# Turning the probabilities of the dilated attention on VectorE and GpSimd instead of TensorE

## The chip, the cores and the metric

One Trainium2 chip, one core. The metric is the device time of one execution in microseconds (us); lower is better. TensorE (PE in the profile), VectorE (DVE), ScalarE (ACT), GpSimd (POOL) and SyncE (SP, which issues the loads of weights) each run a program of their own and meet at semaphores.

## The reference, cut to what matters

Two layers over 256 tokens of width 2048, all in float32: one latent-attention layer (MLA), then one dilated sliding-window layer with three branches (dilation 1, 4, 16) and 16 heads of width 128. The change lies in the second. For each head:

```python
s = jnp.einsum('brnqhe,brnkhe->brnhqk', qs, kb)
s = jnp.where(valid, s * (E ** -0.5) + alibi, NEG_INF)
m = jnp.max(s, axis=-1, keepdims=True)
p = jnp.exp(s - m)
den = jnp.sum(p, axis=-1)
o = jnp.einsum('brnhqk,brnkhe->brnqhe', p, vb) / den
...
wts = jax.nn.softmax(jnp.stack(lses, axis=-1), axis=-1)      # over the three branches
o = jnp.einsum('bshge,bshg->bshe', jnp.stack(outs, axis=3), wts)
return h + (o * jax.nn.silu(gate)) @ w_o
```

The kernel merges the three branches into one softmax over 384 columns per query (256 of the dense branch, 64 of each dilated one), which is the same sum.

## The kernel before, in words

**The bulk.** Nearly all of the time is projections of the 256 tokens by float32 weights. Each weight step (128 x 1024 numbers, 512 KB) is loaded by SP into a ring of four slots, `raw`; ScalarE rounds it to a high part (`highs`, L486), VectorE subtracts to get the low part (`lows`, L837), and TensorE multiplies high and low parts in three matmuls for each product (L1327), 12 matmuls of 512 columns a step. `raw_full`, `hi_ready`, `lo_ready` and `slot_used` carry a slot from engine to engine. Step n + 4 is loaded when step n's low part is done, and rounded when TensorE has used step n.

**The dilated layer.** It runs over 8 pairs of heads, 40 steps (20 "quarters" of two steps) a pair. While pair i is projected, the attention of pair i - 1 runs between its quarters; the attention of the last pair runs between the steps of the output projection, at the steps in `B_LAST_SLOTS`. A pair has four units u (head by 128-query tile). `b_units(s)` says which stage of which unit belongs to quarter s: stage k of unit u in quarter 2 + u + k. So units follow each other one quarter apart, and each has four stages:

- stage 0: TensorE makes the scores (`b_score`, L1571 and L1576) into the bank `score`; VectorE adds the ALiBi table and takes the row maximum (`band_mask`, L929, two instructions of 64 rows, then L934); ScalarE takes the exponential in place in `prob` with the row sum (`unit_exp`, L540);
- stage 1: VectorE takes the reciprocal of the sum (`unit_den`, L965, called by `b_gates` ahead of the quarter's `lows`); ScalarE scales the probabilities (L738); TensorE turns them in three 128x128 blocks into the bank `turn` (`band_turn`, `turn_rows`, L1359); ScalarE copies the bank to `probT` (`unit_turned`, L524);
- stage 2: TensorE multiplies by the values (`band_pv`, L1591 and L1595) at the end of the quarter, ahead of that quarter's turn and score; VectorE multiplies with the gate (`band_out`, L954);
- stage 3: ScalarE and VectorE split the result into high and low part (`band_store` L814, `band_low` L961).

`prob` has two buffers, by u % 2; `probT`, `turn`, `score` and the bank of the product have one.

**The order on each engine** is written out by hand. In quarter s VectorE runs `b_gates`, `lows` of step 4 + 2s, the attention of the quarter (stage 3, 2, 0), the sums and rows of the norms (`chain_sums` L888 and L893, `b_rows` L907), the block turns of queries and keys (L1238), `lows` of step 5 + 2s. ScalarE runs `highs` of step 4 + 2s, the attention, the squares (L517), `highs` of step 5 + 2s. GpSimd has next to nothing: one power for each norm (`chain`, L434; in quarters 3, 7, 11 and 19 of a pair) and once a pair the halving of the ALiBi table (`halve`, L464, quarter 13).

**In the MLA layer** ScalarE carries 16 turned blocks of the keys of each pair to their partitions (L674), in batches that `KEY_MOVES` fixes: so many at MLA step 3, 4, 7 and 8 (step 8 is step 0 of the next pair), the last of which raises `key_turned`. TensorE waits for that in step 3 of the next pair.

Of the kernel before, what the change touches and what calls it, by code (L numbers as in the profile page):

```python
# [76 lines left out]
UNITS = 4  # L77
B_UNIT_0 = UNITS * PAIRS

B_ROUND_0 = 4 + 6 * PAIRS  # L80


def mla_round(i, k):

    return i * 6 - 1 + k
# [20 lines left out]
            for stage in (3, 2, 1, 0) if 0 <= s + 8 * (back - 1) - 3 - stage < UNITS]  # L106


def b_round(i, k):

    return i * UNITS + (B_ROUND_0 - UNITS) + k


QUAD = P // 4


KEY_MOVES = {3: range(0, 3), 4: range(3, 6), 7: range(6, 9), 8: range(9, 16)}


def b_units(s):  # L120
# [40 lines left out]
def build_program(nc, xT, x_later, x_tok, identity, consts, alibis, gains, w_in, w_pe, w_kv, w_gate_first, w_gate, w_q, w_out_a, w_b, w_out_b, out_tok):  # L161
    ctx = ExitStack()
    with ctx:
        def sb(name, shape, dt=F32):
            return ctx.enter_context(nc.sbuf_tensor(name, shape, dt))
# [24 lines left out]
        gate = sb("gate", [P, 2, TILES, 2 * P])  # L190
        rows = sb("rows", [P, 2, TILES, 512])
        prob = sb("prob", [P, 2, 512])
        probT = sb("probT", [P, 512])
        q_ropes = (qT[:, 2 * 512:3 * 512], v[:, 2 * 512:3 * 512])
        og = sb("og", [P, 2, P])
        out = sb("out", [P, 2, P])
# [141 lines left out]
        pv_ready = sem("pv_ready")  # L338
        og_ready = sem("og_ready")
        prob_scaled = sem("prob_scaled")  # L340
        gate_turned = sem("gate_turned")
        og_turned = sem("og_turned")
        o_ready = sem("o_ready")
# [75 lines left out]
        @block.gpsimd  # L419
        def _(pool):  # L420
            nc.gpsimd.memset(mhalf[:], -0.5).then_inc(set_up, 1)
            nc.gpsimd.memset(half[:], 0.5).then_inc(set_up, 1)
            for q_rope in q_ropes:
                nc.gpsimd.memset(q_rope, 0.0).then_inc(set_up, 1)
            pool.wait_ge(set_up, SET_UPS)

            def stream_rms(g):
                pool.wait_ge(x_mean, g + 1)
                nc.gpsimd.tensor_tensor(r[:], x_ms[:], mhalf[:, 0:TILES], ALU.pow).then_inc(r_ready, 1)

            def chain(c, width):

                pool.wait_ge(means, c + 1)
                nc.gpsimd.tensor_tensor(rms[:, 0:width], ms[:, 0:width], mhalf[:, 0:width], ALU.pow)\  # L434
                    .then_inc(rms_ready, 1)


            stream_rms(0)
            chain(0, TILES)
            chain(1, TILES)  # L440

            for i in range(0, PAIRS):
                for s in range(MLA_STEPS):
                    if s == 1:
                        chain(i * 2 + MLA_CHAIN_0, 2 * TILES)
                    if s == 7:
                        chain(i * 2 + (MLA_CHAIN_0 + 1), 2 * TILES)
            pool.wait_ge(loaded, 48)
            pool.sem_inc(alibi_ready, 1)

            def b_pair(i, attend):
                for s in range(B_QUARTERS):
                    if not attend and s == 2:
                        stream_rms(1)
                    for k, (_, at, units) in enumerate(B_CHAINS):
                        if s == at:
                            chain(i * 4 + (B_CHAIN_0 + k), units * TILES)
                    if attend and s == 13:
                        halve(i - 1)

            def halve(i):

                pool.wait_ge(mask_done, i * UNITS + (B_UNIT_0 + UNITS))
                nc.gpsimd.tensor_tensor(phase[:], phase[:], half[:].broadcast_to([P, N_PHASE]), ALU.mult)\  # L464
                    .then_inc(alibi_ready, 1)

            b_pair(0, False)
            for i in range(1, PAIRS):
                b_pair(i, True)


        @block.scalar
        def _(act):
# [252 lines left out]
            def b_attend(i, s):  # L726

                if s == 0:
                    act.wait_ge(blocked, (i - 1) * 4 + 3)
                    gain_of(kT, 2, gn("k_group"))  # L730
                for stage, u in b_units(s):
                    U = (i - 1) * UNITS + (B_UNIT_0 + u)
                    if stage == 3:
                        band_store((i - 1) * UNITS + u, i - 1, u)
                    if stage == 1:
                        act.wait_ge(den_ready, U + 1)
                        at = prob[:, u % 2, 0:BAND]
                        nc.scalar.activation(at, at, ACT.Copy, scale=den_inv[:, u:u + 1]).then_inc(prob_scaled, 1)  # L738
                        unit_turned(b_round(i, u), u, BAND)
                    if stage == 0:  # L740
                        unit_exp(U, u, BAND)

            def query_moves(i, part, parts):

# [87 lines left out]
        def _(dve):  # L832
# [89 lines left out]
            def band_mask(U, B, u, bias, iteration):  # L922

                dve.wait_ge(scored, U + 1)
                if u == 0:
                    dve.wait_ge(alibi_ready, iteration + 1)
                dve.sem_inc(mask_begun, 1)
                for rows_at, first in ((slice(0, HP), P), (slice(HP, P), 0)):
                    last = nc.vector.tensor_tensor_reduce(  # L929
                        out=prob[rows_at, u % 2, 0:BAND], in0=score[rows_at, first:first + BAND], in1=bias[rows_at],  # L930
                        scale=1.0, scalar=-3e38, op0=ALU.add, op1=ALU.max, accum_out=top[rows_at, u:u + 1])
                last.then_inc(mask_done, 1)
                dve.wait_ge(mask_done, U + 1)
                nc.vector.tensor_scalar(top_neg[:, u:u + 1], top[:, u:u + 1], -1.0, None, ALU.mult)\  # L934
                    .then_inc(top_ready, 1)
# [277 lines left out]
                    stream_lows(H_TURNED_AT.index(k - 1))  # L1213
                lows(OUT_A_0 + 4 + k, OUT_A_0 + 4 + k)

            def b_gates(i, s):

                for stage, u in b_units(s):
                    if stage == 1:
                        U = (i - 1) * UNITS + (B_UNIT_0 + u)  # L1220
                        unit_den(U, u)

            def b_blocks(f, k, n):

# [15 lines left out]
            def b_attend(i, s, par_before):  # L1240
                if s == 0:
                    b_rows(i - 1, par_before, 3)
                    dve.wait_ge(rows_ready, i * 4 + B_CHAIN_0)
                    queries = rows[:, 1, :, 0:2 * P]
                    nc.vector.transpose(queries, queries).then_inc(blocked, 1)
                if s in (0, 1):
                    gate_turn(i, s)
                for stage, u in b_units(s):
                    U = (i - 1) * UNITS + (B_UNIT_0 + u)
                    if stage == 3:  # L1250
                        band_low(U, i - 1, u)
                    if stage == 2:
                        band_out(U, i, u)
                    if stage == 0:
                        band_mask(U, (i - 1) * UNITS + u, u, alibi[:, u // 2, u % 2], i - 1)

            def b_rows(i, par, k):
                f, _, units = B_CHAINS[k]
# [7 lines left out]
            def b_pair(i, par, attend):  # L1266
                for s in range(B_QUARTERS):
                    if attend:
                        b_gates(i, s)
                    lows((i, B_STEPS), B_0 + 4 + 2 * s)  # L1270
                    if not attend and s == 1:
                        stream_lows(HALF_FILLS - 2)
# [32 lines left out]
                b_pair(t * 2 + 3, 1, True)  # L1305
            for k in range(OUT_STEPS):
                if k + 1 in B_LAST_SLOTS:
                    b_gates(PAIRS, B_LAST_SLOTS.index(k + 1))
                if k in B_LAST_SLOTS:
                    b_attend(PAIRS, B_LAST_SLOTS.index(k), 1)  # L1310
                if k in OUT_FILL_END:
                    add_stream(OUT_FILL_END.index(k), OUT_B_0, OUT_B_FILL_0, OUT_FILLS)
                if k < OUT_STEPS - 4:
                    lows(OUT_B_0 + 4 + k, OUT_B_0 + 4 + k)
# [3 lines left out]
        def _(pe):  # L1318
# [74 lines left out]

            pe.wait_ge(warm_set, 1)
            for _ in range(WARM):
                nc.tensor.matmul(score[:], probT[:, 0:P], probT[:], start=True, stop=True)
            for n in range(2):
                pe.wait_ge(first_x_hi, n + 1)
                pe.wait_ge(first_hi, n + 1)
# [176 lines left out]
                    last = nc.tensor.matmul(outer, qT[:, col:col + P], kT[:, col:col + P], start=True, stop=True)  # L1576
                last.then_inc(scored, 1)

            def band_turn(U, u, rnd):

                pe.wait_ge(prob_scaled, U - B_UNIT_0 + 1)
                turn_rows(rnd, [(prob[:, u % 2, k * P:(k + 1) * P], k * P) for k in range(BAND // P)])

            def band_pv(U, B, u, rnd):

                h, t = u // 2, u % 2
                pe.wait_ge(turn_read, rnd + 1)
                pe.wait_ge(out_made, B)
                both = probT[:, 0:BAND].rearrange("p (a k) -> p a k", a=2)
                for tile in range(TILES):  # L1590
                    nc.tensor.matmul(pv.rearrange("p (a k) -> p a k", a=2), v[:, tile * 768 + h * P:tile * 768 + (h + 1) * P],  # L1591
                                     both[:, :, tile * P:tile * P + HP], start=tile == 0, stop=False, skip_group_check=True)
                for half, first in ((0, SEQ), (1, HP)):
                    col = t * 768 + (1 + half) * 256 + h * P
                    last = nc.tensor.matmul(pv[:, half * HP:(half + 1) * HP], v[:, col:col + P],  # L1595
                                            probT[:, first:first + HP], start=False, stop=True, skip_group_check=True)
                last.then_inc(pv_ready, 1)

            def b_attend(i, s):
                for stage, u in b_units(s):  # L1600
                    U = (i - 1) * UNITS + (B_UNIT_0 + u)
                    if stage == 2:
                        band_pv(U, (i - 1) * UNITS + u, u, b_round(i, u))
                    if stage == 1:
                        band_turn(U, u, b_round(i, u))
                    if stage == 0:
                        if u == 0:
                            pe.wait_ge(gained, i * 4)
# [147 lines left out]
```

## Time and profile before

| | us |
|---|---|
| median of 3 runs | 1400.31 (1400.23 to 1400.31) |
| the profiled execution, its own time | 1400.47 |
| its span in the trace | 1398.7 |
| PE busy | 1390.0 (99%) |
| DVE busy | 1038.6 (74%) |
| ACT busy | 784.0 (56%) |
| POOL busy | 101.5 (7%) |

The granted clock of TensorE is 1.0, full speed, in all of the span. The profiled execution is 0.16 us above the median, and its span 1.77 us below its own time. In the profile, "L837" is line 837 of the kernel; `w_lo<-raw,w_hi` names output and inputs; "x4" after a row of a timeline counts instructions that are shown as one, and what stands in brackets is the idle time of the engine ahead of it with what ended it. A pair of the dilated layer takes 117.8 us; the rows further down are taken from the pair whose attention lies between 843 and 880 us.

### The profile page before, as it was taken

The numbers are of one execution on the slowest core, as the hardware profiler recorded it, in microseconds if no ns is written. First come the engines' busy times: TensorE is split into PE (matmuls) and PEld (weight loads), VectorE is DVE, ScalarE is ACT, GpSimd is POOL, SyncE is SP. The second block draws the span as 40 slices with busy tenths as digits, with TensorE's granted clock in tenths as the row PEclk, the third lists the DMA queues.
The fourth block names the chain that finished last, engine by engine and source line by source line (L and its number), as shares of the span: only waits on it lengthen the run. The fifth ranks groups of instructions, "written<-read, shape, count | busy, mean of one in ns | idle before, by whom it ended". The sixth has DMA issues, their size and how long they took to land.

```text
span 1398.7 us, 17859 instructions
## 1 busy us (share of the span) xinstructions
PE 1390.0 (99%) x6584; PEld 1162.5 (83%) x6584; DVE 1038.6 (74%) x1825; ACT 784.0 (56%) x1288; POOL 101.5 (7%) x67
## 2 busy tenths in 40 slices
PE   9999999999999999999999999999999999999999
PEld 7888888888888888888888888888888888888787
DVE  6777777757677868777877886887787788688653
ACT  6577777746544654564465465446446545644642
POOL 0101001000010001000101100101010110010000
PEclk9999999999999999999999999999999999999999
DMA  9653444455556545645554654565555465456454
GB/s 356 233 174 133 162 143 140 163 187 177 183 182 211 180 156 178 209 156 180 190 185 149 199 188 157 178 209 166 161 191 192 150 196 194 151 180 198 164 167 149
DMA packets 71223, 252.40 MB, mean 180 GB/s; under 512 B 7904, under 2 KB 8288, under 8 KB 71136
## 3 DMA queue, kind: packets, MB, share of 16 engines
q1 hardware_dynamic: 70704, 249.95, 54.2%
q10 hardware_dynamic: 432, 1.31, 0.3%
q8 instruction: 52, 0.85, 0.2%
q14 instruction: 35, 0.29, 0.1%
HBM read 249.14 MB, written 2.10 MB: 180 GB/s over the span
## 4 chain that ended last, share of the span: by engine, by line
PE 94%; DVE 3%; ACT 2%; issue 1%; DMA 1%; SPq 0%; POOL 0%; DVEq 0%; ACTq 0%
PE acc L1327 86%; PE turn L1359 1%; PE score L1576 1%; DVE w_lo L837 1%; PE score L1571 1%; PE pv_bank L1591 1%; PE pv_bank L1371 1%; DVE ss L888 1%; PE score L1467 1%; PE score L1469 1%; PE pv_bank L1595 1%; DVE prob L929 1%; ACT rows L517 1%; DMA raw<-in_w_in 1%; ACT prob L738 0%
## 5 line engine op out<-in xcount | busy, mean ns | idle before, releaser
L837 DVE TENSOR_TENSOR w_lo<-raw,w_hi 128x1024 fp32r<-128x1024 f32 x463 | 573.3, 1248 | 201.9 <-ACT w_hi L486 198.0
L486 ACT ACTIVATE w_hi<-raw 128x1024 fp32r<-128x1024 f32 x463 | 482.3, 1050 | 363.4 <-PE acc L1327 355.3
L1327 PE MATMUL acc<-w_hi,xa_hi 128*128 128x512 f32 x956 | 378.5, 396 | 0.4 <-DVE w_lo L837 0.3
L1327 PE MATMUL acc<-w_hi,xa_lo 128*128 128x512 f32 x956 | 373.0, 390 | 0.0
L1327 PE MATMUL acc<-w_lo,xa_hi 128*128 128x512 f32 x956 | 372.6, 390 | 0.0
L1327 PE MATMUL acc<-w_hi,xb_hi 128*128 128x512 f32 (+1 forms) x640 | 249.5, 390 | 0.0
L1327 PE MATMUL acc<-w_hi,xb_lo 128*128 128x512 f32 (+1 forms) x640 | 245.9, 384 | 0.0
L1327 PE MATMUL acc<-w_lo,xb_hi 128*128 128x512 f32 (+1 forms) x640 | 245.6, 384 | 0.0
L1327 PEld LDWEIGHTS acc<-w_hi,xa_lo 128*128 128x128 f32 x956 | 179.4, 188 | 37.7
L1327 PEld LDWEIGHTS acc<-w_hi,xa_hi 128*128 128x128 f32 x956 | 179.7, 188 | 37.3 <-issue 0.9
L1327 PEld LDWEIGHTS acc<-w_lo,xa_hi 128*128 128x128 f32 x956 | 179.7, 188 | 35.8
L434 POOL TENSOR_TENSOR rms<-ms,mhalf 128x4 f32<-128x4 f32 (+2 forms) x50 | 73.1, 1462 | 1048.6 <-DVE ms L893 854.7
L1327 PEld LDWEIGHTS acc<-w_hi,xb_lo 128*128 128x128 f32 x640 | 120.1, 188 | 22.7
L1327 PEld LDWEIGHTS acc<-w_lo,xb_hi 128*128 128x128 f32 x640 | 120.3, 188 | 22.1
L1327 PEld LDWEIGHTS acc<-w_hi,xb_hi 128*128 128x128 f32 x640 | 120.3, 188 | 21.9
L1327 PE MATMUL acc<-w_hi,oT_hi 128*128 128x512 f32 x256 | 102.3, 400 | 0.0
L1327 PE MATMUL acc<-w_hi,oT_lo 128*128 128x512 f32 x256 | 100.0, 391 | 0.0
L1327 PE MATMUL acc<-w_lo,oT_hi 128*128 128x512 f32 x256 | 99.8, 390 | 0.0
L1238 DVE STREAM_TRANSPOSE kT<-rows 32x256 f32<-32x256 f32 (+1 forms) x256 | 94.5, 369 | 4.5
L540 ACT ACTIVATE prob<-prob,top_neg 128x128 f32<-128x128 f32 (+1 forms) x64 | 34.3, 536 | 93.0 <-DVE top_neg L934 70.9
L517 ACT ACTIVATE rows<-acc 128x512 f32<-128x512 f32 (+2 forms) x50 | 39.2, 783 | 34.3 <-PE acc L1327 34.0
L929 DVE CUSTOM_DVE_ANT_0 prob<-score,phase 64x384 f32<-64x384 f32 x64 | 35.5, 555 | 29.8 <-PE score L1576 29.4
(179 smaller groups left out, 1163.6 us busy)
## 6 DMA issues: line engine op xcount, KB each, us to landing
raw<-in_w_b SPq DMA_DIRECT2D x320, 512.0 KB, 3.8
raw<-in_w_out_a SPq DMA_DIRECT2D x32, 512.0 KB, 3.3
raw<-in_w_out_b SPq DMA_DIRECT2D x32, 512.0 KB, 3.3
raw<-in_w_gate SPq DMA_DIRECT2D x30, 512.0 KB, 3.6
raw<-in_w_kv SPq DMA_DIRECT2D x16, 512.0 KB, 4.3
raw<-in_w_in SPq DMA_DIRECT2D x15, 512.0 KB, 6.2
raw<-in_w_q SPq DMA_DIRECT2D x16, 384.0 KB, 3.0
res<-in_x_tok SPq DMA_DIRECT2D x4, 512.0 KB, 7.9
```

What stands on the lines that cost most here:

```text
L434: nc.gpsimd.tensor_tensor(rms[:, 0:width], ms[:, 0:width], mhalf[:, 0:width], ALU.pow)\
L486: nc.scalar.activation(w[0][:, s, 0:width], raw[:, s, 0:width], ACT.Copy).then_inc(hi_ready, 1)
L517: nc.scalar.activation(rows[:, buf, :, 0:width], acc[:, pair, :, 0:width], ACT.Square)\
L540: nc.scalar.activation(prob[:, u % 2, 0:width], prob[:, u % 2, 0:width], ACT.Exp, bias=top_neg[:, u:u + 1], accum_out=den[:, u:u + 1])\
L837: nc.vector.tensor_tensor(w[1][:, s, 0:width], raw[:, s, 0:width], w[0][:, s, 0:width].bitcast(F32), ALU.subtract).then_inc(lo_ready, 1)
L888: nc.vector.tensor_reduce(ss[:, 0, 0:n].rearrange("p (t u) -> p t u", t=TILES), rows[:, buf, :, 0:units * span].rearrange("p t (u d) -> p ...
L929: last = nc.vector.tensor_tensor_reduce(out=prob[rows_at, u % 2, 0:BAND], in0=score[rows_at, first:first + BAND], in1=bias[rows_at], scale ...
L1238: return nc.vector.transpose(dst, src)
L1327: last = nc.tensor.matmul(out, x(a), y(b), start=start and k == 0, stop=stop and k == 2, **more)
L1359: last = nc.tensor.transpose(turn[:, col:col + P], src, ident[:])
L1371: last = nc.tensor.matmul(pv, probT[:, k * P:(k + 1) * P], val, start=k == 0, stop=k == len(values) - 1)
L1467: nc.tensor.matmul(score[:, 0:n], qT[:, par * 512 + at:par * 512 + at + P], kT[:, k_0 + h * SEQ:k_0 + h * SEQ + n], start=True, stop=False)
```

## The change

The three transposes on TensorE and ScalarE's copy of their bank go. The reciprocal (`unit_den`) and the scaling move from stage 1 to stage 0, right behind the exponential. At the start of quarter 3 + u VectorE turns the 32x32 blocks of the unit's 128x384 probabilities in place (`prob_turns`), and GpSimd carries the turned blocks from `prob` to `probT` in 16 copies of 32 partitions x 96 elements (`prob_moves`), each from one group of 32 partitions to another. `probT` gets two buffers. `band_pv` waits for the copies (`prob_moved`), and so does the mask of the unit after next, which writes the same buffer of `prob`. GpSimd's copies stand ahead of the power of quarter 3. Apart from that, the batches of key moves in the MLA layer are cut anew: 1, 3, 4 and 8 blocks instead of 3, 3, 3 and 7.

```diff
-KEY_MOVES = {3: range(0, 3), 4: range(3, 6), 7: range(6, 9), 8: range(9, 16)}
+KEY_MOVES = {3: range(0, 1), 4: range(1, 4), 7: range(4, 8), 8: range(8, 16)}
...
-        probT = sb("probT", [P, 512])
+        probT = sb("probT", [P, 2 * BAND])
...
             def b_pair(i, attend):                       # GpSimd
                 for s in range(B_QUARTERS):
+                    for stage, u in b_units(s) if attend else ():
+                        if stage == 1:
+                            prob_moves(i, u)
...
                         if s == at:
+                            if attend and k < 2:
+                                pool.wait_ge(prob_moved, (i - 1) * UNITS + (1, UNITS)[k])
                             chain(i * 4 + (B_CHAIN_0 + k), units * TILES)
...
+            def prob_moves(i, u):
+
+                B = (i - 1) * UNITS + u
+                pool.wait_ge(rms_ready, i * 4 + B_CHAIN_0 + (1 if u and i < PAIRS else 0))
+                pool.wait_ge(prob_blocks, B + 1)
+                pool.wait_ge(pv_ready, B_UNIT_0 + B - 1)
+                tiles = prob[:, u % 2, 0:BAND].rearrange("p (t k) -> p t k", k=P)
+                turned = probT[:, u % 2 * BAND:(u % 2 + 1) * BAND].rearrange("p (t k) -> p t k", k=P)
+                for n in range(16):
+                    a, b = n // 4, n % 4
+                    last = nc.gpsimd.tensor_copy(turned[b * QUAD:(b + 1) * QUAD, :, a * QUAD:(a + 1) * QUAD],
+                                                 tiles[a * QUAD:(a + 1) * QUAD, :, b * QUAD:(b + 1) * QUAD])
+                last.then_inc(prob_moved, 1)
...
-                    if stage == 1:                       # ScalarE
+                    if stage == 0:
+                        unit_exp(U, u, BAND)
                         act.wait_ge(den_ready, U + 1)
                         at = prob[:, u % 2, 0:BAND]
                         nc.scalar.activation(at, at, ACT.Copy, scale=den_inv[:, u:u + 1]).then_inc(prob_scaled, 1)
-                        unit_turned(b_round(i, u), u, BAND)
-                    if stage == 0:
-                        unit_exp(U, u, BAND)
...
                 dve.wait_ge(scored, U + 1)               # VectorE, band_mask
                 if u == 0:
                     dve.wait_ge(alibi_ready, iteration + 1)
+                if B >= 2:
+                    dve.wait_ge(prob_moved, B - 1)
...
-            def b_gates(i, s):
+            def prob_turns(i, s):
 
                 for stage, u in b_units(s):
                     if stage == 1:
-                        U = (i - 1) * UNITS + (B_UNIT_0 + u)
-                        unit_den(U, u)
+                        dve.wait_ge(prob_scaled, (i - 1) * UNITS + u + 1)
+                        nc.vector.transpose(prob[:, u % 2, 0:BAND], prob[:, u % 2, 0:BAND]).then_inc(prob_blocks, 1)
...
                         band_mask(U, (i - 1) * UNITS + u, u, alibi[:, u // 2, u % 2], i - 1)
+                        unit_den(U, u)
...
-            def band_turn(U, u, rnd):                    # TensorE
-
-                pe.wait_ge(prob_scaled, U - B_UNIT_0 + 1)
-                turn_rows(rnd, [(prob[:, u % 2, k * P:(k + 1) * P], k * P) for k in range(BAND // P)])
-
-            def band_pv(U, B, u, rnd):
+            def band_pv(U, B, u):
 
                 h, t = u // 2, u % 2
-                pe.wait_ge(turn_read, rnd + 1)
+                pe.wait_ge(prob_moved, B + 1)
                 pe.wait_ge(out_made, B)
```

## Rows read from the trace of the kernel before

**Rows 1.** The page, part 1: busy time, share of the span and instructions of each engine.
```profile
PE 1390.0 (99%) x6584; PEld 1162.5 (83%) x6584; DVE 1038.6 (74%) x1825; ACT 784.0 (56%) x1288; POOL 101.5 (7%) x67
```

**Rows 2.** Waits of PE: us in total, times, longest us.
```profile
PE turn L1359 <- ACT prob L738: 3.3, 8, 1.7
```

**Rows 3.** Timeline of PE, one pair's attention: start us, us, engine, line, operation, idle.
```profile
856.13 0.61 PE L1591 MATMUL pv_bank<-probT,v 128*128 128x128 f32 x4
...
857.35 0.55 PE L1359 MATMUL turn<-ident,prob 128*128 128x128 f32 x3 [0.22 <-ACT prob L738]
...
864.11 0.61 PE L1591 MATMUL pv_bank<-probT,v 128*128 128x128 f32 x4
...
864.95 0.50 PE L1359 MATMUL turn<-ident,prob 128*128 128x128 f32 x3
865.28 0.60 PE L1571 MATMUL score<-kT,qT 128*128 128x256 f32 x2
...
871.65 0.61 PE L1591 MATMUL pv_bank<-probT,v 128*128 128x128 f32 x4
...
878.32 0.61 PE L1591 MATMUL pv_bank<-probT,v 128*128 128x128 f32 x4
```

**Rows 4.** Timeline of DVE in the same pair.
```profile
844.33 0.55 DVE L929 CUSTOM_DVE_ANT_0 prob<-score,phase 64x384 f32<-64x384 f32 x1 [0.54 <-PE score L1576]
...
863.17 0.15 DVE L965 RECIPROCAL den_inv<-den 128x1 f32<-128x1 f32 x1
863.24 1.20 DVE L837 TENSOR_TENSOR w_lo<-raw,w_hi 128x1024 fp32r<-128x1024 f32 x1
864.37 0.28 DVE L961 TENSOR_TENSOR oT_lo<-out,oT_hi 128x128 fp32r<-128x128 f32 x1
...
866.51 0.55 DVE L929 CUSTOM_DVE_ANT_0 prob<-score,phase 64x384 f32<-64x384 f32 x1 [1.07 <-PE score L1576]
...
869.57 1.23 DVE L837 TENSOR_TENSOR w_lo<-raw,w_hi 128x1024 fp32r<-128x1024 f32 x1 [1.73 <-ACT w_hi L486]
```

**Rows 5.** Timeline of ACT in the same pair.
```profile
863.36 0.62 ACT L738 ACTIVATE prob<-prob,den_inv 128x384 f32<-128x384 f32 x1 [0.22 <-DVE den_inv L965]
...
867.88 0.62 ACT L540 ACTIVATE prob<-prob,top_neg 128x384 f32<-128x384 f32 x1 [1.90 <-DVE top_neg L934]
...
868.50 1.99 ACT L486 ACTIVATE w_hi<-raw 128x1024 fp32r<-128x1024 f32 x2
```

**Rows 6.** Timelines of POOL and DVE around the halving of the ALiBi table (L464).
```profile
903.69 1.23 DVE L837 TENSOR_TENSOR w_lo<-raw,w_hi 128x1024 fp32r<-128x1024 f32 x1
...
903.81 3.71 POOL L464 TENSOR_TENSOR phase<-phase,half 128x1536 f32<-128x1536 f32 x1
...
905.00 3.60 DVE L837 TENSOR_TENSOR w_lo<-raw,w_hi 128x1024 fp32r<-128x1024 f32 x1
```

**Rows 7.** Timeline of POOL: two memsets at the start, three powers in the same pair.
```profile
0.77 0.10 POOL L422 MEMSET half<- 128x1 f32 x1
0.81 0.53 POOL L424 MEMSET qT<- 128x512 f32 x1
...
855.52 2.55 POOL L434 TENSOR_TENSOR rms<-ms,mhalf 128x8 f32<-128x8 f32 x1 [25.92 <-DVE ms L893]
881.14 1.64 POOL L434 TENSOR_TENSOR rms<-ms,mhalf 128x8 f32<-128x8 f32 x1 [23.07 <-DVE ms L893]
902.84 1.01 POOL L434 TENSOR_TENSOR rms<-ms,mhalf 128x4 f32<-128x4 f32 x1 [20.06 <-DVE ms L893]
```

**Rows 8.** Groups of DVE, shapes apart: count | busy us, mean ns | idle before.
```profile
L1245 DVE STREAM_TRANSPOSE rows<-rows 128x512 f32<-128x512 f32 x8 | 5.7, 711 | 0.3
```

**Rows 9.** Timeline of PE in the last pair, beside the output projection.
```profile
1338.80 0.61 PE L1591 MATMUL pv_bank<-probT,v 128*128 128x128 f32 x4
...
1342.75 0.61 PE L1591 MATMUL pv_bank<-probT,v 128*128 128x128 f32 x4
```

**Rows 10.** Groups of ACT, shapes apart: count | busy us, mean ns | idle before.
```profile
L674 ACT ACTIVATE kT<-rows 32x128 f32<-32x128 f32 x128 | 39.3, 307 | 1.7
```

More of the change, by code:

```diff
@@ L78 @@
 B_UNIT_0 = UNITS * PAIRS
-B_ROUND_0 = 4 + 6 * PAIRS
 def mla_round(i, k):
@@ L106, in mla_units @@
             for stage in (3, 2, 1, 0) if 0 <= s + 8 * (back - 1) - 3 - stage < UNITS]
-def b_round(i, k):
-    return i * UNITS + (B_ROUND_0 - UNITS) + k
 QUAD = P // 4
-KEY_MOVES = {3: range(0, 3), 4: range(3, 6), 7: range(6, 9), 8: range(9, 16)}
+KEY_MOVES = {3: range(0, 1), 4: range(1, 4), 7: range(4, 8), 8: range(8, 16)}
 def b_units(s):
@@ L340, in build_program @@
         prob_scaled = sem("prob_scaled")
+        prob_blocks = sem("prob_blocks")
+        prob_moved = sem("prob_moved")
         gate_turned = sem("gate_turned")
@@ L469, in _ @@
                 b_pair(i, True)
+            for u in range(UNITS):
+                prob_moves(PAIRS, u)
         @block.scalar
@@ L1268, in b_pair @@
                     if attend:
-                        b_gates(i, s)
+                        prob_turns(i, s)
                     lows((i, B_STEPS), B_0 + 4 + 2 * s)
@@ L1307, in _ @@
                 if k + 1 in B_LAST_SLOTS:
-                    b_gates(PAIRS, B_LAST_SLOTS.index(k + 1))
+                    prob_turns(PAIRS, B_LAST_SLOTS.index(k + 1))
                 if k in B_LAST_SLOTS:
@@ L1395, in _ @@
             for _ in range(WARM):
-                nc.tensor.matmul(score[:], probT[:, 0:P], probT[:], start=True, stop=True)
+                nc.tensor.matmul(score[:], probT[:, 0:P], probT[:, 0:512], start=True, stop=True)
             for n in range(2):
@@ L1577, in b_score @@
                 last.then_inc(scored, 1)
-            def band_turn(U, u, rnd):
-                pe.wait_ge(prob_scaled, U - B_UNIT_0 + 1)
-                turn_rows(rnd, [(prob[:, u % 2, k * P:(k + 1) * P], k * P) for k in range(BAND // P)])
-            def band_pv(U, B, u, rnd):
+            def band_pv(U, B, u):
                 h, t = u // 2, u % 2
-                pe.wait_ge(turn_read, rnd + 1)
+                pe.wait_ge(prob_moved, B + 1)
                 pe.wait_ge(out_made, B)
-                both = probT[:, 0:BAND].rearrange("p (a k) -> p a k", a=2)
+                turned = probT[:, u % 2 * BAND:(u % 2 + 1) * BAND]
+                both = turned.rearrange("p (a k) -> p a k", a=2)
                 for tile in range(TILES):
@@ L1595, in band_pv @@
                     last = nc.tensor.matmul(pv[:, half * HP:(half + 1) * HP], v[:, col:col + P],
-                                            probT[:, first:first + HP], start=False, stop=True, skip_group_check=True)
+                                            turned[:, first:first + HP], start=False, stop=True, skip_group_check=True)
                 last.then_inc(pv_ready, 1)
@@ L1602, in b_attend @@
                     if stage == 2:
-                        band_pv(U, (i - 1) * UNITS + u, u, b_round(i, u))
-                    if stage == 1:
-                        band_turn(U, u, b_round(i, u))
+                        band_pv(U, (i - 1) * UNITS + u, u)
                     if stage == 0:
```

## The prediction, made before the changed kernel was run

> **What bounds the kernel now.** I began with the busy shares [rows 1]: PE is busy in 99% of the span, DVE in 74%, ACT in 56%, POOL in 7%. A busy PE is only a bound if it never waits, so the waits of PE came next [rows 2]: beside start-up, the one thing it waits for in 1398.7 us is the scaled probabilities ahead of a transpose, 8 times, 3.3 us in all, 1.7 of them once. The kernel is bound by TensorE's own work, and an instruction taken from PE shortens it, as long as nothing else becomes late. Then I read PE's, DVE's and ACT's timelines over one pair [rows 3 to 5], to price the transposes and to see when each step of a unit would be ready.
>
> **What goes.** On PE a unit's transposes take from 864.95 to the score at 865.28, 0.33 us, every other unit alike [rows 3]. There are 32 units: 28 in the seven pairs that run beside the next pair's projection give 28 x 0.33 = 9.2 us. In each of these pairs one transpose also waits 0.22 us (857.35) [rows 3], 7 x 0.22 = 1.5 us, which goes too. In the last pair the same removes 4 x 0.33 and the wait of 1.7 [rows 2], 3.0 us, but see the tail below. ScalarE's copy of the bank also goes, from an engine that has room.
>
> **What is late next.** PE's multiplication by the values, which now waits for GpSimd. One turn of a unit on PE is 864.11 to 871.65, 7.54 us; without the transposes 7.21 [rows 3].
>
> The ring on DVE and ACT, in starts. Mask to exponential 866.51 to 867.88, 1.37; exponential and read of its sum to reciprocal some 0.77 (0.62 and an estimate for the read); reciprocal to scaling 863.17 to 863.36, 0.19; scaling to ScalarE's next rounding 0.54 (its 0.62 less the usual overlap); a rounding to the low part it releases 868.50 to 869.57, 1.07; low part to DVE's next instruction 863.24 to 864.37, 1.13 [rows 4, 5]. Then comes the new block turn. The nearest row is the in-place turn of 128x512 in 711 ns [rows 8]; three quarters of it is 0.53, and I take 0.5 start to start; 0.71 is the upper end, which would shift the copies by 0.2. Then the low part of the next step, 1.13. So the copies can start 6.7 us after the unit's mask. With the 0.2 and 0.25 of `band_low` and `band_out` the ring closes in 7.2 us, which is just PE's 7.21: DVE doesn't fall behind, but it has nothing to spare in these quarters.
>
> Why the copies start only behind that low part: GpSimd and VectorE exclude each other here. One L837 takes 1.23 us; the next, issued at 905.00 while `halve` runs on POOL, takes 3.60, and `halve`, issued at 903.81 under the first, takes 3.71 [rows 6]. Ends fit one owner at a time: first L837 to 904.92, `halve` to 907.52, second L837 1.1 us on. The power of 855.52 takes 2.55 against 1.64 at 881.14 in the same way [rows 7]. After the block turn DVE goes straight into L837, so POOL waits.
> The Trainium skill ("SBUF — State Buffer", Who interferes with whom) says that a VectorE instruction with two SBUF inputs excludes a GpSimd one that reads SBUF, and one with a single such input does not. By that rule the copies would not slow masks, sums and block turns; if these were blocked too, each would wait one copy, 0.2 us, some 0.6 a unit in a ring without room, and three such units in each of 8 pairs would take back the whole gain. No row here tests this with a burst of copies.
>
> **The price of a copy.** No row shows one. Lower bound: the memsets start 0.04 apart and the 128x512 one takes 0.53, so 0.83 ns an element; 96 elements give 0.04 + 0.08 = 0.12 us [rows 7]. Upper: the powers of 4 and 8 columns take 1.01 and 1.64, 0.16 a column and 0.38 fixed [rows 7]; with `halve`'s 2.60 us for 1536 elements (1.7 ns each) [rows 6] a copy is 0.38 + 0.16 = 0.54. The nearest row is `halve`, plain arithmetic that reads SBUF: twice the memset's 0.83 x 1536 is 2.55 of its 2.60, so a reading instruction has a small fixed cost. I take 0.04 for dispatch, 0.08 for writing and as much for the read ahead of it, 0.20, and 16 x 0.20 = 3.2 us a unit; ends 1.9 and 8.6.
> The Trainium skill ("GPSIMD Engine Reference", Performance pitfalls) gives about 102 cycles for each read command that doesn't overlap the one before; an estimate by it is 0.21 us a copy, 3.3 a unit.
>
> **Does it fit?** Window from the earliest start of the copies to PE's need:
> - u0: mask 844.33, start 851.0; PE at 856.13 - 0.33 = 855.8: 4.8 us.
> - u1: mask 851.0; the squares, sums and means of the norm add 1.3, start 859.1. PE at 855.8 + 7.21 = 863.0: 3.9.
> - u2: mask 859.3, start 866.0; PE at 870.2: 4.2, less a collision with `band_low`.
> - u3: mask 866.5, start 873.2; PE at 870.2 + (878.32 - 871.65 - 0.33) = 876.5: 3.3 [rows 3, 4].
> 3.2 us fit everywhere, the last by a hair. No stall.
> Of the other waits: the power of quarter 3 now stands behind unit 0's copies (done 854.2; its means come at 856.3), hidden up to 5.3 us of copies; behind it wait DVE's L907 and all later `lows`. The mask's wait for the unit before last costs nothing at this size. The low part of 869.57 comes about 0.9 later, since scaling now precedes it; PE wants it at 871.65 + 1.17 + 2.7 = 875.5, so 4 us of cover remain; without it that 0.9 would be paid three times a pair. The halving is in quarter 13, clear of the copies. Key moves: as many as before, the last batch one longer, 0.31 us [rows 10], three steps ahead of PE's need: nothing; uncovered, 8 x 0.31 = 2.5. SP issues nothing new.
>
> **Tail.** In the last pair one step, not two, lies between the products of units 2 and 3: 1338.80 to 1342.75 [rows 9]. The window of 3.3 loses 2.7 and PE stalls 2.6 to 2.9, which eats that pair's 3.0. Net 0.1.
>
> **Sum:** 9.2 + 1.5 + 0.1 = 10.8 us off the profiled execution's 1400.47; the median is 0.16 lower, 1400.31, so 1389.5 to 1389.7: I say **1389.6**. With the lower bound of the copy the tail gives 1.2 more, 1388.4; with none of it in the way, 1387.
>
> **Rivals.**
> 1. *Copies somewhat dearer, 0.25 us (4.0 a unit).* u1 stalls 0.2, u3 0.6; 7 x 0.8 + 0.8 = 6.4; 1396. A reading instruction's fixed cost could be larger than `halve` lets through, since part of it may hide under the wait for the port.
> 2. *GpSimd becomes the bound: slower.* The place is PE's wait for `prob_moved` ahead of L1591. The point of decision is some 0.29 us a copy (4.6 a unit), where stalls eat the gain. At 0.30: 7 x 1.65 + 1.6 = 13.2, 1402.7. At 0.35 the copies of u1 run into the next L837 and lose 1.1 more: about 4 a pair, 31 in all, 1421. At the bound of 0.54 each unit takes 8.6 and two such collisions, some 18 a pair, 1530. For it: the powers' 0.38 fixed. Against: `halve`.
> 3. *The port is not handed over fairly.* If a burst of 16 keeps it, `band_low` and with it the mask wait up to 3.2 us and not 0.2. DVE's ring has no room, so the stall recurs at u2 and u3: 2 x 3 x 8 = 48, 1438. If instead each collision costs DVE 0.2 to 0.3, three times a pair, 7 us: 1397. Rows 6 show one owner after another, which speaks for turns.
> 4. *No effect:* the transposes' slots hid under weight loads. PE's starts are 0.33 later because of them [rows 3], so hardly.
>
> **How the numbers follow.** The forecast (copy up to 0.22) has 0.55; rival 1 and the mild form of 3 together 0.13; rival 2 0.24; rival 3's hard form 0.04; no effect 0.04. A measurement of this kernel can tell about 0.2% (2.8 us) from no change. Faster: 0.55 + 0.11 = 0.66; same: 0.02 of rivals 1 and 3, 0.01 of 2 at just 0.29, and 0.04, so 0.07; slower 0.27. The likeliest case's own range is 1387 to 1392. The range reaches from 1387 into rival 2 up to a copy of 0.35, 1421, leaving out about 0.17.
>
> **What would show it.** PE without L1359 in the dilated layer; L1591 with no wait but in the last pair; a pair of 116.3 instead of 117.8 us; POOL's group of 32x96 copies x512 at about 0.2 us start to start; L837 beside a copy longer by no more than one copy. Wrong if PE waits for POOL in every pair, or if DVE's masks start later each unit.

## The result and the profile after

The changed kernel takes 1431.67 us (median of 4 runs, 1430.06 to 1434.52) against 1400.28 before: ratio 1.0226, 95% interval 1.0212 to 1.024. It is 31 us slower; I had forecast 11 us faster and a range up to 1421. The profiled execution took 1430.06, its span is 1428.3.

First the shares of the engines and the page's costliest group on POOL, which was not there before [rows 1]:

```profile
PE 1396.4 (98%) x6488; PEld 1160.7 (81%) x6488; DVE 1056.9 (74%) x1857; ACT 768.0 (54%) x1256; POOL 277.2 (19%) x579
...
L470 POOL COPY probT<-prob 32x96 f32<-32x96 f32 x512 | 176.2, 344 | 206.4 <-issue 186.0
```

PE has 96 instructions fewer and is "busy" for longer; POOL is idle four fifths of the time. Neither share tells what happened. The waits of PE do (us in total, times, longest in us):

```profile
PE pv_bank L1603 <- POOL probT L470: 26.3, 16, 3.5
PE score L1412 <- POOL v L418: 1.8, 1, 1.8
PE acc L1343 <- DVE w_lo L850: 0.2, 1, 0.2
```

Where PE used to wait 3.3 us for the scaled probabilities [rows 2], it now waits 26.3 for the last copy of a unit. Next, PE's timeline over one pair, the first product by the values of each of the four units, as in [rows 3]:

```profile
865.31 0.71 PE L1603 MATMUL pv_bank<-probT,v 128*128 128x128 f32 x4
...
874.49 0.71 PE L1603 MATMUL pv_bank<-probT,v 128*128 128x128 f32 x4 [1.68 <-POOL probT L470]
...
883.48 0.61 PE L1603 MATMUL pv_bank<-probT,v 128*128 128x128 f32 x4
...
890.72 0.71 PE L1603 MATMUL pv_bank<-probT,v 128*128 128x128 f32 x4 [0.73 <-POOL probT L470]
```

The steps are 9.18, 8.99 and 7.24, where 7.97, 7.55 and 6.67 stood before and 7.21, 7.21 and 6.34 were forecast. The second step has no wait and is still 1.8 us too long; its cause is another one and comes below. POOL's timeline in the same pair shows why unit 1 and unit 3 are late (the rows with x16 are one unit's copies):

```profile
859.61 5.64 POOL L470 COPY probT<-prob 32x96 f32<-32x96 f32 x16 [20.47 <-issue]
866.06 2.49 POOL L428 TENSOR_TENSOR rms<-ms,mhalf 128x8 f32<-128x8 f32 x1 [0.81 <-DVE ms L906]
868.61 5.83 POOL L470 COPY probT<-prob 32x96 f32<-32x96 f32 x16
874.61 5.64 POOL L470 COPY probT<-prob 32x96 f32<-32x96 f32 x16 [0.17 <-issue]
883.11 7.55 POOL L470 COPY probT<-prob 32x96 f32<-32x96 f32 x16 [2.86 <-issue]
```

Unit 1's copies start at 868.61 behind the power and end at 874.44; PE goes on at 874.49. L850 is the subtraction for the low part, L837 before the change. Here are single copies of unit 1, and the L850 that one of them meets, in POOL's and DVE's timelines:

```profile
871.01 0.26 POOL L470 COPY probT<-prob 32x96 f32<-32x96 f32 x1
871.31 0.26 POOL L470 COPY probT<-prob 32x96 f32<-32x96 f32 x1
...
872.82 1.31 POOL L470 COPY probT<-prob 32x96 f32<-32x96 f32 x1
...
872.78 1.22 DVE L850 TENSOR_TENSOR w_lo<-raw,w_hi 128x1024 fp32r<-128x1024 f32 x1 [0.38 <-ACT w_hi L501]
```

A copy takes 0.26 us and the next starts 0.30 after its start. One that meets L850 takes 1.31, about 1.05 more, while L850 keeps its 1.22. So a unit takes 16 x 0.30 = 4.8 us and about 1 for each L850 it meets: one in unit 1, and three in unit 3, whose first copy is issued under an L850 (7.55 in all; the three copies concerned take 0.85, 0.92 and 0.98 more than 0.26).

The long second step is TensorE's clock. The rows are stretches of 1 us of this pair: their length, PE's busy time, the number of matmuls, the granted clock as a share of 2.4 GHz, and the DMA share with GB/s:

```profile
872.00:873.00 1.00, 0.81 (x4) 1.00 0.00 0
873.00:874.00 1.00, 0.00 (x0) 1.00 0.00 0
874.00:875.00 1.00, 0.51 (x4) 1.00 0.03 12
875.00:876.00 1.00, 1.00 (x8) 0.86 0.94 303
876.00:877.00 1.00, 1.00 (x6) 0.50 0.87 262
877.00:878.00 1.00, 1.00 (x4) 0.50 0.78 209
878.00:879.00 1.00, 1.00 (x4) 0.50 0.66 246
879.00:880.00 1.00, 1.00 (x5) 0.93 0.08 33
```

PE stood still for 1.68 us, up to 874.49; from 875.72 on the granted clock was 1.2 and not 2.4 GHz, for 3.4 us, which costs 1.7. Over the whole execution there are six such stretches of 3.4 us in the seven overlapped pairs and one of 6.8 around the last pair's first product, 27.3 us at half speed, some 13.5 us lost. The kernel before had none.

Put together, from the first product of the first pair to that of the last pair it is 844.2 us against 820.9 before, 23.3 more. With half the copies, the first experiment below, it is 806.8, so the transposes with the waits ahead of them were worth 14.0 there. The low clock adds 10.2. The remaining 27.1 are stalls of PE. Its waits for the copies hold 22.9 of them (without the last unit's), and a stall costs some 0.3 more than the idle time shown (the step of 9.18 is 1.94 over 7.24 with a wait of 1.68), which for 15 stalls fits the other 4.2. From the last pair's first product to the end it is 5.8 more than before, and 0.4 more up to the first product: 29.6 in all, the difference of the spans.

### The profile page after: what moved, and what is told of

It is laid out like the page before. It is cut to its first block, busy times and chain, and to the rows that moved or that the text cites. A ratio compares the mean times of both kernels' runs of the same rounds, so it can differ in the third digit from the quotient of the medians.

```text
span 1428.3 us, 18200 instructions
## 1 busy us (share of the span) xinstructions
PE 1396.4 (98%) x6488; PEld 1160.7 (81%) x6488; DVE 1056.9 (74%) x1857; ACT 768.0 (54%) x1256; POOL 277.2 (19%) x579
## 3 DMA queue, kind: packets, MB, share of 16 engines
q10 hardware_dynamic: 432, 1.31, 0.2%
## 4 chain that ended last, share of the span: by engine, by line
PE 79%; DVE 7%; POOL 6%; issue 4%; ACT 3%; DMA 1%; SPq 0%; DVEq 0%; ACTq 0%; POOLq 0%
PE acc L1343 73%; POOL probT L470 6%; DVE prob L944 2%; DVE w_lo L850 2%; ACT prob L555 1%; ACT w_hi L501 1%; PE pv_bank L1603 1%; PE pv_bank L1387 1%; DVE ss L901 1%; PE score L1483 1%; PE score L1485 1%; PE score L1592 1%; ACT rows L532 1%; PE score L1587 1%; DVE prob L1236 1%
## 5 line engine op out<-in xcount | busy, mean ns | idle before, releaser
L850 DVE TENSOR_TENSOR w_lo<-raw,w_hi 128x1024 fp32r<-128x1024 f32 x463 | 573.5, 1248 | 199.1 <-ACT w_hi L501 195.1
L1343 PE MATMUL acc<-w_hi,xa_hi 128*128 128x512 f32 x956 | 382.6, 400 | 0.4 <-DVE w_lo L850 0.2
L470 POOL COPY probT<-prob 32x96 f32<-32x96 f32 x512 | 176.2, 344 | 206.4 <-issue 186.0
```

Of the source, the lines that this page charges most:

```text
L470: last = nc.gpsimd.tensor_copy(turned[b * QUAD:(b + 1) * QUAD, :, a * QUAD:(a + 1) * QUAD], tiles[a * QUAD:(a + 1) * QUAD, :, b * QUAD:(b ...
L850: nc.vector.tensor_tensor(w[1][:, s, 0:width], raw[:, s, 0:width], w[0][:, s, 0:width].bitcast(F32), ALU.subtract).then_inc(lo_ready, 1)
L1343: last = nc.tensor.matmul(out, x(a), y(b), start=start and k == 0, stop=stop and k == 2, **more)
```

## The experiments

Before the runs I held **theory G** (G for GpSimd): only the copies' price was wrong, and everything follows from when their last one lands. **Rival R**: the ring of VectorE and ScalarE is the bound, since scaling and block turn now stand ahead of the low parts; then shorter copies help little.

### Half the copies

```diff
-                for n in range(16):
+                for n in range(0, 16, 2):
```

> The changed kernel with every second one of the 16 copies left out (half of the turned probabilities don't reach probT), all waits kept. Theory G (GpSimd's copies are the bound: 16 x 0.301 us start to start, 4.8 a unit, against windows of 3.9 and 3.3, each collision with L850 adding about 1 us): 8 x 0.30 = 2.4 us fit every window but the last pair's, PE doesn't wait for POOL in the first seven pairs, the granted clock stays 1.0 there, and the time is 1400.3 - 10.8 + 1.0 for the key moves - 0.8 for the shorter tail = about 1389.7 (1388 to 1391.5). Rival R (the ring of VectorE and ScalarE is the bound, since scaling and block turn now stand ahead of the low parts): half the copies change little of it, PE still waits in each pair, and the time stays above 1405.

Measured: **1390.98 us**, ratio 0.9933 (0.9919 to 0.9947). PE's timeline over the pair, then POOL's for units 1 and 3:

```profile
851.42 0.61 PE L1603 MATMUL pv_bank<-probT,v 128*128 128x128 f32 x4
...
858.66 0.61 PE L1603 MATMUL pv_bank<-probT,v 128*128 128x128 f32 x4
...
865.90 0.61 PE L1603 MATMUL pv_bank<-probT,v 128*128 128x128 f32 x4
...
872.25 0.61 PE L1603 MATMUL pv_bank<-probT,v 128*128 128x128 f32 x4
```

```profile
854.72 2.37 POOL L470 COPY probT<-prob 32x96 f32<-32x96 f32 x8
...
867.83 3.22 POOL L470 COPY probT<-prob 32x96 f32<-32x96 f32 x8 [3.88 <-issue]
```

The steps are 7.24, 7.24 and 6.35, within 0.03 of the forecast's 7.21, 7.21, 6.34. PE has no wait for the copies in seven pairs, and a pair takes 116.04 us against 117.77: the transposes and what hung on them are worth 1.73 a pair. The last pair stalls 3.1 us and then has 3.4 us at the low clock, some 1.6 us that this expectation had not counted and that account for the 1.3 above its 1389.7. Rival R falls: block turn, early scaling and all waits are as in the changed kernel, and PE never waits for them.

### Early scaling alone

The kernel before, with the reciprocal (VectorE) and the scaling (ScalarE) in stage 0; TensorE still turns.

```diff
-                    if stage == 1:
-                        act.wait_ge(den_ready, U + 1)
-                        ...scaling...
-                        unit_turned(b_round(i, u), u, BAND)
-                    if stage == 0:
-                        unit_exp(U, u, BAND)
+                    if stage == 1:
+                        unit_turned(b_round(i, u), u, BAND)
+                    if stage == 0:
+                        unit_exp(U, u, BAND)
+                        act.wait_ge(den_ready, U + 1)
+                        ...scaling...
...
                         band_mask(U, (i - 1) * UNITS + u, u, alibi[:, u // 2, u % 2], i - 1)
+                        unit_den(U, u)
```

> The kernel before with one part of the change alone: reciprocal and scaling in stage 0, right behind the exponential; TensorE still turns. Theory G: early scaling costs PE nothing and takes away the 8 waits of 3.3 us ahead of the transposes: about 1397.0 (1396 to 1398.5). Rival R: the later low parts make PE wait for L837, 1403 or more.

Measured: **1395.04 us**, ratio 0.9963 (0.9949 to 0.9976). It is faster by 5.3 and not by 3.3, below the range: a pair takes 117.31 instead of 117.77, so what shows as a wait of 0.22 us had cost 0.46, and in the same way the last pair's wait of 1.7 had cost 2.0 (from the seventh pair's first product to the last pair's it is 111.85 us instead of 114.27, and 0.46 of the difference is the seventh pair's own). This part of the change is a gain by itself, clear of the interval.

### The form of the copies, pair by pair

Pair 3 has four copies of 128x96, all partitions at once and each staying where it is; the other pairs change form or number:

```diff
+                if i == 3:
+                    for n in range(4):
+                        last = nc.gpsimd.tensor_copy(turned[:, :, n * QUAD:(n + 1) * QUAD], tiles[:, :, n * QUAD:(n + 1) * QUAD])
+                for n in {2: range(16), 3: (), 4: range(16), 5: range(1), 6: range(12), 7: range(8)}.get(i, range(16)):
...
+                    if i == 2:
+                        last = nc.gpsimd.tensor_copy(dst[:, 0], src[:, 0])
+                    elif i == 4:
+                        last = nc.gpsimd.memset(dst, 0.0)
```

> The changed kernel with another form of the copies in each pair (its output isn't the reference's from pair 2 on): pair 2 only a third of each copy (32x32), pair 3 four copies of 128x96 within the partitions, pair 4 memsets of 32x96 in their place, pair 5 one copy, pair 6 twelve, pair 7 eight, pairs 1 and 8 as they are. Prices, start to start: if the fixed part is what I mis-sized (0.04 assumed), 32x32 takes about 0.25 and 128x96 the same 0.30 as 32x96; if it is the rate, 32x32 takes 0.10 to 0.15. Memsets, which read nothing, take 0.12 each and don't wait for L850 if only the read port is shared; if they do wait, the first is about 1.1 us long. Pairs 5 and 7 run with no wait of PE for POOL and take 116.3 us between equal points; pair 6 (3.6 a unit) waits under 1 us in all; pairs 2 (4.0) and 6 thus lie between. Rival R: all pairs take about 120.5.

Measured: 1408.99 us (one run). POOL's timeline for unit 1, behind the power, of pairs 2, 3 and 4, then pair 5's one copy in unit 0 (issued under an L850) and in unit 1 (not), and pair 6's unit 3:

```profile
626.97 3.90 POOL L475 COPY probT<-prob 32x32 f32<-32x32 f32 x16
...
746.98 0.90 POOL L470 COPY probT<-prob 128x96 f32<-128x96 f32 x4
...
863.03 3.30 POOL L477 MEMSET probT<- 32x96 f32 x16
...
970.07 1.11 POOL L479 COPY probT<-prob 32x96 f32<-32x96 f32 x1 [20.46 <-issue]
...
979.07 0.26 POOL L479 COPY probT<-prob 32x96 f32<-32x96 f32 x1
...
1108.22 6.45 POOL L479 COPY probT<-prob 32x96 f32<-32x96 f32 x12 [2.66 <-issue]
```

32x32 costs 0.244 start to start and 32x96 0.301: 0.9 ns an element and 0.215 us besides, where I had assumed 1.7 ns and 0.04 us. That split holds for copies of 32 partitions. The copies of 128x96, which stay in their partitions and move four times as much each, start 0.21 apart, each before the one ahead has ended (0.27), and not the 0.30 that I expected: the same 128x384 numbers go in 0.90 us and not in 4.8. The change of partitions isn't what costs: of a unit's 16 copies four (those with a = b) stay in their group, and in the changed kernel these too start 0.30 apart from their neighbours. So the price hangs on the number of instructions, and on the 32 rows of each.

The memset of 32x96 takes 0.206, not the 0.12 that I had built from two memsets at the start [rows 7]; and its 16 take 3.30 us in every unit of pair 4, also where they begin under L850, while the one copy of pair 5 in that place takes 1.11. So what reads SBUF waits for L850, and what only writes does not. The Trainium skill ("SBUF — State Buffer", Who interferes with whom) says just this: a VectorE instruction with two SBUF inputs contends with a GpSimd one that reads SBUF, and not with one that only writes it. The trace agrees, with 1.11 us for the copy and 3.30 for the 16 memsets.

Pairs 3, 4 and 5 (and 7, with eight copies) have PE's steps of 7.24, 7.24, 6.35. Pair 6, with twelve, has 7.24, 7.24, 8.43: only unit 3 is late, by 2.1 us and not by the under 1 that I expected, since its copies meet three L850 (6.45 us for twelve). Pair 2 waits at unit 3 too (2.0 us).

### ScalarE carries a part

The whole computation again. GpSimd takes blocks 7 to 15, ScalarE 0 to 6 in its idle time ahead of the next exponential; key moves as before the change. The semaphore `prob_carried` is new; TensorE and the mask wait for it as well.

```diff
+                    if stage == 1:                       # ScalarE
+                        act.wait_ge(prob_blocks, B + 1)
+                        act.wait_ge(pv_ready, B_UNIT_0 + B - 1)
+                        for n in range(7):
+                            ... nc.scalar.activation(turned[...], tiles[...], ACT.Copy)
+                        last.then_inc(prob_carried, 1)
```

> The whole computation: ScalarE carries 7 of a unit's 16 blocks in its idle time ahead of the next exponential, GpSimd 9; key moves as before the change. Theory G: GpSimd 9 x 0.30 = 2.7 us, ScalarE 7 x 0.3 = 2.1 us beside it, both inside 3.3; PE waits in the last pair alone; 1400.3 - 10.8 - 0.5 = about 1389 (1387.5 to 1391), faster than the kernel before. Rival R: ScalarE is in the ring, so that its copies make it longer: slower than 1400. A middle case, ScalarE's copies delaying each exponential by some 0.2 us: 1391 to 1394.

Measured: **1393.20 us**, ratio 0.995 (0.9937 to 0.9962), faster than the kernel before but 2.2 us above its range. The steps are 7.24, 7.24 and 6.62, so ScalarE's copies make no step of units 0 to 2 longer. Unit 3 is late: it shows as a wait of 0.12 and costs 0.40 a pair (116.44 against 116.04 with half the copies), 7 x 0.40 = 2.8. The last pair stalls 3.4 us and has 3.4 us at the low clock. POOL's row for unit 3:

```profile
868.05 4.64 POOL L471 COPY probT<-prob 32x96 f32<-32x96 f32 x9 [3.55 <-issue]
```

4.64 for nine where three other units take at most 3.56: the ninth copy meets the next L850 and takes 1.35. With eight (3.24 in the version below) it is 1.4 us less.

### ScalarE carries half, and TensorE turns the last pair

```diff
-                        for n in range(7):
+                        for n in range(8):
...
+                if B >= UNITS * (PAIRS - 1):             # last pair: band_turn as before the change
+                    pe.wait_ge(turn_read, LAST_ROUND_0 + u + 1)
```

> The whole computation, three edits on the changed kernel: ScalarE carries 8 of a unit's 16 blocks and GpSimd 8; the last pair is turned on TensorE as before the change, with early scaling; key moves as before the change. Theory G: in the first seven pairs no wait of PE for the copies and 116.04 us a pair, as with half the copies, against 117.77 before (7 x 1.73 = 12.1 off); the last pair as with early scaling alone (2.4 off and units 2 and 3 again 3.95 apart): 1400.4 - 14.5 = 1385.9 (1385 to 1388). If ScalarE's eighth block delays the exponentials: 0.1 to 0.2 a unit more, up to 1390. Rival R: over 1395.

Measured: **1386.28 us** (1386.26 to 1386.32, 4 runs), ratio 0.9899 (0.9884 to 0.9914): 14.0 us faster than the kernel before and inside its range. The first fence has PE's waits over the whole span, the second one, from its timeline, three of the last pair's products:

```profile
PE score L1424 <- POOL v L420: 1.8, 1, 1.8
```

```profile
1317.11 0.61 PE L1624 MATMUL pv_bank<-probT,v 128*128 128x128 f32 x4
...
1324.66 0.61 PE L1624 MATMUL pv_bank<-probT,v 128*128 128x128 f32 x4
...
1328.61 0.61 PE L1624 MATMUL pv_bank<-probT,v 128*128 128x128 f32 x4
```

Only the wait at the start is left, each pair takes 116.04 (the seventh 110.93 up to the last pair's first product), the last product comes 3.95 behind the one before it as in [rows 9], and the clock stays at 2.4 GHz.

### All 16 on GpSimd, but one quarter earlier

VectorE's block turn right behind the scaling (where VectorE waits for ScalarE's rounding anyway), GpSimd's copies moved up accordingly; key moves as before the change.

```diff
                         unit_den(U, u)
+                        dve.wait_ge(prob_scaled, (i - 1) * UNITS + u + 1)
+                        nc.vector.transpose(...).then_inc(prob_blocks, 1)
```

> The changed kernel (all 16 copies on GpSimd, last pair too) with VectorE's block turn moved from the next quarter to right behind the scaling, where VectorE waits for ScalarE's rounding anyway, and GpSimd's copies one quarter earlier in its order (those of unit 1 ahead of the power of quarter 3); key moves as before the change. Theory G, by which only the place between the copies' start and PE's need matters: the copies start about 3.2 us earlier, run into two L850 each (4.8 + 2 x 1.0 = 6.8 us) and fit units 0 to 2; unit 3 stalls up to 1 us, the last pair 3 us and its clock: 1392 to 1397, so most of the changed kernel's loss of 31 us goes with no copy removed. If GpSimd's sheer load or the collisions were the cause, the time would stay over 1415.

Measured: **1424.04 us**, ratio 1.0171 (1.0156 to 1.0186), against 1431.67; far over my 1392 to 1397, and over the 1415 beyond which I had said that load or collisions would be the cause. POOL's rows in the pair are units 0 and 1 together, the power, unit 2 and unit 3; then comes PE's wait:

```profile
856.39 13.48 POOL L470 COPY probT<-prob 32x96 f32<-32x96 f32 x32 [18.38 <-issue]
869.95 1.64 POOL L428 TENSOR_TENSOR rms<-ms,mhalf 128x8 f32<-128x8 f32 x1
871.65 6.68 POOL L470 COPY probT<-prob 32x96 f32<-32x96 f32 x16
879.21 8.52 POOL L470 COPY probT<-prob 32x96 f32<-32x96 f32 x16 [0.88 <-issue]
```

```profile
887.78 0.92 PE L1594 MATMUL pv_bank<-probT,v 128*128 128x128 f32 x4 [2.63 <-POOL probT L470]
```

Units 0 to 2 took the 6.7 us that I had reckoned, and PE's first two steps are 7.24 and 7.24: unit 1's stall is gone. Unit 3 takes 8.52, since behind the last mask VectorE issues four L850, two and two, and the copies meet them all; PE loses 2.8 (a step of 9.14 against 6.35) in every pair. From the first copy at 879.21 to where PE would have gone on without a stall, 885.0, are 5.8 us. The 4.8 us of the copies alone would have fit, and the 3.7 us of collisions did not. So the place explains unit 1 and the collisions explain unit 3; neither part of the expectation holds whole.

The pairs also give the price of the clock, their stalls being alike: pairs 2 and 5 with no stretch of low clock take 118.96, pairs 1 and 4 with one of 3.4 us 120.5, pairs 3 and 6 with one of 6.8 us 121.9 and 122.1.

The same with the last pair turned on TensorE:

> As e6, and the last pair turned on TensorE. Theory G: the last pair's stall and its low clock go, 4 to 6 us less than e6: 1387 to 1392.

Measured: 1419.11 us, ratio 1.013 (1.0113 to 1.0147). That is 4.9 less than the version before it, within the 4 to 6, but not a clean reading of the last pair: the profiled executions take 1422.11 and 1422.52, and the one of this version, with no stall in its last pair, has 34 us at the low clock where the other has 27. The total misses by the same error at unit 3.

### Key moves alone

```diff
-KEY_MOVES = {3: range(0, 1), 4: range(1, 4), 7: range(4, 8), 8: range(8, 16)}
+KEY_MOVES = {3: range(0, 3), 4: range(3, 6), 7: range(6, 9), 8: range(9, 16)}
```

> The changed kernel with the batches of key moves as before the change. All theories: the dilated layer begins 1.0 us earlier (first product by the values at 502.3 and not 503.3 us); the rest as in the changed kernel, 1430 to 1432, if the phase of the low-clock stretches stays; they may shift it by some us.

Measured: 1429.86 us (one run). The first product comes at 502.96, only 0.3 earlier, because this execution was 0.6 later early on: the MLA layer's first product by the values comes at 103.3 us and not at 102.7. Free of the start, from the first to the last of the 96 products by the values in the MLA layer (`pv_bank<-v,probT`) there are 200.6 us here, 200.5 before the change and 201.5 in the changed kernel; the other traces say 201.6 with the new batches (two) and 200.5 to 200.6 with the old (five). In the stalls of the weight loads there, PE's wait for the exponential ahead of a transpose is 1.7 us (6 times) with the new batches and 0.6 (3 times) with the old. The new batches cost 0.9 to 1.0 us.

## Why the prediction was wrong

- **What bounds the kernel** (PE's own work) and **what the transposes are worth** held: 1.54 a pair forecast, 1.73 with half the copies. The surplus is that a wait of 0.22 cost 0.46. The masks beside the copies didn't get longer either (0.54 and 0.56, as before), as the prediction expected.
- **The ring of VectorE and ScalarE** held: with 8 copies PE's steps are within 0.03 of those I wrote down. The windows held as well: with 8 copies a unit, from their start (or, for units 0, 2 and 3, from the end of the L850 that holds up the first copy by 3.22 - 2.37 = 0.85) to PE's product, they are 4.9, 3.9, 4.3 and 3.6 us against 4.8, 3.9, 4.2 and 3.3.
- **The failed step is the price of a copy.** The prediction took 0.20 us, with a "small fixed cost" read off `halve`; it is 0.30, and 0.215 of that hang on no element. 16 copies take 4.8 us and not 3.2, against windows of 3.9 and 3.3, so "No stall" became two stalls a pair. Its second estimate, 0.21, was as short. From this alone rival 2 is the case, and its sum at 0.30 said 1402.7. That `halve` hid a fixed part under its wait for the port, as rival 1 had allowed, fits, but no run shows it; the measured 0.215 lies midway between the 0.04 that was taken and the powers' 0.38.
- **The sum at 0.30 was too low even by its own windows.** 4.8 against 3.9 and 3.3 gives stalls of 0.9 and 1.5, 2.4 a pair; the prediction has 1.65 and doesn't say why.
- **The collisions were mis-sized too.** At 0.30 the copies of unit 1 end at 863.9, and by the prediction's own ring the next L850 starts at 863.2; it costs 1.05, which the prediction counts only from 0.35 on. For unit 3 it starts the copies behind one L850 and has none after it; there are two more. So the stalls are 1.9 and 1.8 in the pairs in which the clock stays up between them, and some 24 us over seven pairs against 7 x 1.65 = 11.6.
- **The clock was missing from the sum.** I read it as 1.0 throughout, and took a stall to cost its own length. Some 13.5 us more went that way. This, the 12 of the stalls and about 2 in the last pair lead from 1402.7 to 1431, beyond the 1421 that I had allowed for 0.35. That the result lies only 10 us above the range is no merit of the range, which had no term for the clock.
- **Key moves**, costed at nothing, cost 0.9 to 1.0 us.
- **Rival 3 (the port not handed over fairly)** came out the other way round: VectorE loses next to nothing. L850 took 558.3 us in all against 558.0 for the same 447 before; GpSimd's copies bear the collisions. `band_low` went from 0.28 to 0.33.
- **The tail** as forecast eats the last pair's gain: unit 3 stalls 3.1 us with half the copies, and not at all in the version that turns the last pair on TensorE. In the changed kernel it stalls 3.45, and unit 0 of that pair, for which the prediction had no stall, another 2.7: its 16 copies take 6.57 us there.

Two questions stay open: whether fewer, wider copies across partition groups are possible at all, and what decides in which pairs the clock falls. In the changed kernel's second pair it didn't, with stalls of 1.68 and 1.64 us as in other pairs, nor after the last unit's stall of 3.45. No run has the changed kernel with 16 copies free of collisions or with the clock held up, so the shares of price, collisions and clock in its 31 us are worked out from rows and not measured one by one.

## What to carry to other kernels

When work moves from a saturated engine to an idle one, price it by the count of instructions first: sixteen copies of 32x96 took 4.8 us, only 1.4 of it for the elements, and four copies of 128x96 with the same data 0.90. Then lay it between the moment it can start and the moment it is wanted, unit by unit, with each collision at a shared port counted where it falls; idle share (POOL was idle 81% of the time) says nothing. A stall of 1.7 us on the otherwise never idle TensorE was followed in some pairs by another 1.7 lost to the clock, so a schedule that fits with nothing to spare should be given less work: 8 copies on each of two engines instead of 16 on one, with the last pair left to TensorE, turned a loss of 31 us into a gain of 14.

## What the runs showed of the hardware

- A 32x96 float32 copy took GpSimd 0.26 us, 0.301 start to start, whether it stayed in its group of partitions or not; 32x32 0.244; a memset of 32x96 0.206, though two small memsets in a row at the kernel's start stand 0.04 apart; a 128x96 copy within its partitions 0.21. ScalarE's 32x96 copy takes 0.28.
- A GpSimd copy that meets a 128x1024 subtraction of two SBUF tensors on VectorE waits for its end (up to 1.31 us instead of 0.26), the subtraction loses nothing measurable, and a memset doesn't wait.
- TensorE's granted clock fell from 2.4 to 1.2 GHz for 3.4 or 6.8 us around stalls of 1.6 to 3.5 us amid dense work, in most pairs and not in all: after a stall of 2.63 us in 12 of 14 pairs (the two versions one quarter earlier), in six of the changed kernel's first seven pairs with stalls of 1.6 to 1.7, and not beside stalls of 0.8 us or less. Each 3.4 us at the low clock cost about 1.6 us.
- A stall costs PE some 0.2 to 0.3 us more than the idle time that the profile shows: 0.22 shown and 0.46 lost, 1.68 shown and 1.94 lost, 0.12 shown and 0.40 lost.
